# Two transformer blocks on one core: loads in order of use, squares spread out, a short norm, and the last updates shared with TensorE

## What is computed

```python
def rms_norm(x, g):                       # also rmsnorm
    y = xf * lax.rsqrt(jnp.mean(xf * xf, axis=-1, keepdims=True) + EPS)
    return y * g

h = x                                     # first block
hn = rms_norm(h, norm_g[0]); proj = hn @ w_in; ...
x = rms_norm(h, final_g)                  # end of the first block
xn = rmsnorm(x, norm_mix_pre)             # start of the second: two norms in a row
...
x = x + rmsnorm(mix_out, norm_mix_post)   # "the middle" below
hn = rmsnorm(x, norm_ffn_pre)
u = square(relu(hn @ w_up)); y = u @ w_down
x = x + rmsnorm(y, norm_ffn_post)         # the end
```

## Time and profile before

| what | value |
|---|---|
| median of 3 runs | 2653.14 us (2651.64 to 2653.33) |
| the profiled execution, its own time | 2653.11 us |
| its span | 2651.1 us |
| TensorE busy | 2606.0 us, 98% of the span |
| VectorE, ScalarE, GpSimd busy | 1609.6, 1217.0, 25.9 us |
| chain of work that ended last | TensorE 93%, VectorE 3%, ScalarE 1%, transfers 1% |

### The profile page before, as it was taken

How to read it: one execution, slowest core, us unless ns; L and a number is a source line. 1 busy time by engine, 2 the same in 40 slices (tenths; PEclk the granted TensorE clock), 3 DMA queues, 4 the chain that set the end, 5 groups by cost and what they waited for, 6 DMA issues and landing times.

```text
span 2651.1 us, 29862 instructions
## 1 busy us (share of the span) xinstructions
PE 2606.0 (98%) x11725; PEld 2160.2 (81%) x11725; DVE 1609.6 (61%) x1868; ACT 1217.0 (46%) x1471; POOL 25.9 (1%) x49
## 2 busy tenths in 40 slices
PE   7999999999999999999999999999999999999997
PEld 6888888888888888887888888888878888888886
DVE  4545665566657666766866666555576565565565
ACT  5554443444454444455444444444454344344443
POOL 1000000000000000000000000000000000000000
PEclk9999999999999999999999999999999999999999
DMA  6666766676765555677555666666657666676773
GB/s 216 206 193 194 212 197 198 193 212 195 220 201 174 170 166 166 191 227 210 160 181 176 182 183 183 200 198 207 216 161 220 196 203 215 188 218 206 200 221 121
DMA packets 437933, 515.39 MB, mean 194 GB/s; under 512 B 198416, under 2 KB 200576, under 8 KB 437792
## 3 DMA queue, kind: packets, MB, share of 16 engines
q1 hardware_dynamic: 434320, 504.45, 62.9%
q0 software_dynamic: 2384, 6.93, 1.0%
q10 hardware_dynamic: 1088, 2.10, 0.2%
HBM read 488.24 MB, written 2.10 MB: 185 GB/s over the span
## 4 chain that ended last, share of the span: by engine, by line
PE 93%; DVE 3%; ACT 1%; DMA 1%; issue 1%; SPq 1%; DVEq 0%; ACTq 0%
PE bank L33 92%; PE bank L36 1%; DMA t_stage<-in_a_w_in_dram 1%; DVE t_wl L51 1%; SPq L72 1%; DMA t_ytl<-t_pool 0%; ACT t_wh L42 0%; DVE t_pool L39 0%; ACT t_junk L42 0%; DVE t_pool L51 0%; DVE t_hres L54 0%; ACT t_pool L42 0%; DVE t_rq L51 0%; ACT t_yth L42 0%; DMA t_xtl<-t_pool 0%
## 5 line engine op out<-in xcount | busy, mean ns | idle before, releaser
L51 DVE TENSOR_TENSOR t_wl<-t_stage,t_wh 128x1024 fp32r<-128x1024 f32 x914 | 1102.6, 1220 | 694.7 <-ACT t_wh L42 693.1
L42 ACT ACTIVATE t_wh<-t_stage 128x1024 fp32r<-128x1024 f32 x914 | 953.6, 1056 | 839.7 <-PE bank L33 827.9
L33 PE MATMUL bank<-t_wl,t_xth 128*128 128x512 f32 x2496 | 989.1, 396 | 12.1 <-DVE t_xtl L54 6.3
L33 PE MATMUL bank<-t_wh,t_xtl 128*128 128x512 f32 x2496 | 975.8, 391 | 0.0
L33 PE MATMUL bank<-t_wh,t_xth 128*128 128x512 f32 x2496 | 975.0, 391 | 0.0
L33 PEld LDWEIGHTS bank<-t_wl,t_xth 128*128 128x128 f32 x2496 | 470.8, 189 | 108.6 <-DVE t_wl L51 7.0
L33 PEld LDWEIGHTS bank<-t_wh,t_xtl 128*128 128x128 f32 x2496 | 470.3, 188 | 99.6
L33 PEld LDWEIGHTS bank<-t_wh,t_xth 128*128 128x128 f32 x2496 | 471.0, 189 | 94.9 <-issue 0.2
L33 PE MATMUL bank<-t_wl,t_yth 128*128 128x512 f32 x1024 | 399.1, 390 | 0.0
L33 PE MATMUL bank<-t_wh,t_yth 128*128 128x512 f32 x1024 | 398.6, 389 | 0.0
L33 PE MATMUL bank<-t_wh,t_ytl 128*128 128x512 f32 x1024 | 398.5, 389 | 0.0
(11 more groups left out here) (185 smaller groups left out, 970.7 us busy)
## 6 DMA issues: line engine op xcount, KB each, us to landing
t_stage<-in_a_w_in_dram SPq DMA_DIRECT2D x192, 512.0 KB, 4.1
t_stage<-in_w_in_dram SPq DMA_DIRECT2D x178, 512.0 KB, 4.3
t_stage<-in_b_w_in_dram SPq DMA_DIRECT2D x128, 512.0 KB, 3.7
t_stage<-in_w_up_dram SPq DMA_DIRECT2D x128, 512.0 KB, 4.0
t_stage<-in_w_down_dram SPq DMA_DIRECT2D x128, 512.0 KB, 4.3
t_stage<-in_a_w_out_dram SPq DMA_DIRECT2D x64, 512.0 KB, 4.5
t_ytl<-t_pool SPq DMA_DIRECT2D x128, 128.0 KB, 3.2
t_stage<-in_b_w_out_dram SPq DMA_DIRECT2D x32, 512.0 KB, 5.3
```

What stands on the lines that cost most here:

```text
L33: return lambda e: e.matmul(*a, **k)
L42: return lambda e: e.activation(*a, **k)
L51: return lambda e: e.tensor_tensor(*a, **k)
```

## The change

It has four parts.

1. *Opening.* x is loaded by SyncE, its four pieces between the first five groups, each ahead of the groups that need it. TensorE gets four matmuls on a zeroed tile at the very start and three behind the first two turns (`busy_matmuls`); ScalarE gets one tiny copy at the start. Splits are issued one group ahead until group 5, then two, three, four (`ahead`). Group 0 begins with its four high x high matmuls, which need only the high part of the weights. The eight squares of x are four pieces; the first chunk's evacuation is a piece too. The 1 MB table is loaded behind the split of group 8.
2. *End of the first block.* Both norms come from one chain on four columns instead of two chains on two.
3. *Middle and end.* The last group of the last chunk does its six matmuls for i = 0 first, then those for i = 1 (`halves`), so that the half's square can start. Three chunks' sums are added up ahead (`partial_sum`); `short_norm` takes ScalarE's Sqrt, VectorE's reciprocal and one Newton step. Seven and five matmuls on constants follow the last real ones. In the middle, x is updated in pieces of 256 columns, and TensorE begins the next chunk when two pieces are turned instead of four.
4. *The last updates.* GpSimd has none. Three (i = 1 of columns 0, 1, 2) are made by TensorE: ahead of the last chunk it copies x into accumulators with three matmuls against the identity, and behind the norm it adds the sum times a diagonal matrix of the scale; ScalarE copies the results out. The other five stay on VectorE. The output goes in eight transfers of 256 KB, one of them from ScalarE's queue.

```diff
+    blank = pool4[:, 3, 0, 0:256]
+    c_blank = DV.do(lambda e: e.memset(blank, 0.0))
+    AC.do(lambda e: e.activation(junk[:, 0:64], blank[:, 0:64], ACT.Copy), c_blank)
+    def busy_matmuls(n):
+        for _ in range(n):
+            PE.run(lambda e: e.matmul(mbank[1][:, 0:256], blank[:, 0:128], blank, start=True, stop=True), c_blank)
...
-    for j in range(N_STAGE):
-        load_group(j)
+    load_group(0)
+    load_x(1)
+    load_group(1)
+    load_group(2)
+    load_x(2)
+    load_group(3)
+    load_group(4)
+    load_x(3)
+    def ahead(j):
+        return j + min(AHEAD, max(1, j - 4))
...
-            advance(j + AHEAD)
+            advance(ahead(j))
+            if j == 0:
+                need(lambda: 0 in ready and 1 in ready)
+                PE.wait(split_hi[0], *ready[0])
+                for kk in range(2):
+                    for i in range(2):
+                        PE.run(lambda e, o=acc[2 * pair + i], h=tokens(xh, kk, i), w=wh[:, 0, kk, :], f=kk == 0:
+                               e.matmul(o, h, w, start=f, stop=False))
+                PE.wait(split[0])
...
+            by_half = halves is not None and g == nk // 2 - 1
+            steps = [(kk, i) for i in range(2) for kk in range(2)] if by_half else \
+                [(kk, i) for kk in range(2) for i in range(2)]
...
+    def partial_sum(x, sums, n, width, marks):
+        m = DV.do(lambda e: e.tensor_reduce(x, sums[:, :, 0:n], AX, ALU.add), *marks)
+        return DV.do(lambda e: e.tensor_scalar(x, x, 1.0 / width, EPS, ALU.mult, ALU.add), m)
+    def short_norm(dst, x, part, last, width, marks):
+        a = rq[:, 0, 0:2]
+        m = DV.do(lambda e: e.scalar_tensor_tensor(out=x, in0=last, scalar=1.0 / width, in1=part,
+                                                   op0=ALU.mult, op1=ALU.add), *marks)
+        m = AC.do(lambda e: e.activation(a, x, ACT.Sqrt), m)
+        m = DV.do(lambda e: e.reciprocal(dst, a), m)
+        m = DV.do(lambda e: e.tensor_tensor(a, dst, x, ALU.mult), m)
+        m = DV.do(lambda e: e.scalar_tensor_tensor(out=a, in0=a, scalar=-0.5, in1=dst, op0=ALU.mult,
+                                                   op1=ALU.mult), m)
+        return DV.do(lambda e: e.scalar_tensor_tensor(out=dst, in0=a, scalar=1.5, in1=dst, op0=ALU.add,
+                                                      op1=ALU.mult), m)
...
-    pump()
-    pump()
+    turns[0]()
+    split_group(0)
+    load_group(5)
+    turns[1]()
+    busy_matmuls(2)
+    pool4_clear = PE.do(lambda e: e.matmul(mbank[1][:, 0:256], blank[:, 0:128], blank, start=True, stop=True))
+    temps.free[3] = (pool4_clear,)
+    later(*turns[2:])
...
-    later(x_norm)
+    later((x_square(0), 3), x_square(1), x_square(2), x_square(3), x_scale, first_evac)
...
-        m = norm_scale(s1, None, ssq, 4, D, (sq,))
-        m = DV.do(lambda e: e.tensor_tensor(s11, s1, s1, ALU.mult), m)
-        x2s = rq[:, 1, 2:4]
-        m = DV.do(lambda e: e.tensor_reduce(x2s, ssq2[:, :, 0:4], AX, ALU.add), m, sq2)
-        m = DV.do(lambda e: e.tensor_tensor(x2s, x2s, s11, ALU.mult), m)
-        m = DV.do(lambda e: e.tensor_scalar(x2s, x2s, 1.0 / D, EPS, ALU.mult, ALU.add), m)
-        m = rsqrt(s2, x2s, 2, (m,))
-        m = DV.do(lambda e: e.tensor_tensor(s12, s1, s2, ALU.mult), m)
+        m = DV.do(lambda e: e.tensor_reduce(v1, ssq[:, :, 0:4], AX, ALU.add), sq)
+        m = DV.do(lambda e: e.tensor_scalar(v1, v1, 1.0 / D, EPS, ALU.mult, ALU.add), m)
+        m = DV.do(lambda e: e.tensor_scalar(eps1, v1, EPS, None, ALU.mult), m)
+        m2 = DV.do(lambda e: e.tensor_reduce(v12, ssq2[:, :, 0:4], AX, ALU.add), sq2)
+        m = DV.do(lambda e: e.scalar_tensor_tensor(out=v12, in0=v12, scalar=1.0 / D, in1=eps1, op0=ALU.mult,
+                                                   op1=ALU.add), m, m2)
+        m = rsqrt(s12_1, both, 4, (m,))
...
+        if c == 3:
+            warm_n, warm, warm_free = misc.take()
+            for _ in range(7):
+                PE.run(lambda e: e.matmul(warm[:, 0:256], neg[:, 0:128], mask, start=True, stop=True), c_neg, c_mask,
+                       *warm_free)
...
+            if q == 3 and c == 2:
+                for n, (cc, i) in enumerate(by_pe):
+                    b = (tbank + mbank)[n]
+                    summed[cc, i] = b
+                    PE.run(lambda e, b=b, cc=cc, i=i: e.matmul(b, ident, hres[:, i, cols(cc)], start=True, stop=False),
+                           *trans.free[0], *trans.free[1], *misc.free[0], *misc.free[1], *sqf)
...
+    for _ in range(5):
+        PE.run(lambda e: e.matmul(acc[0][:, 0:256], neg[:, 0:128], mask, start=True, stop=True), *acc_free[0])
+    m_sD = short_norm(sD, xD, partD, ssq[:, :, 3], D, (sqd[-1], m_part))
...
+    for c, i in by_pe:
+        mm = PE.do(lambda e, c=c, i=i: e.matmul(summed[c, i], diag[:, i, :], drs[c][:, i, :], start=False, stop=True),
+                   m_diag[i], dr_marks[c, i])
+        d = dacc[:, i, cols(c)]
+        ready_out[c, i] = d, AC.do(lambda e, c=c, i=i, d=d: e.activation(d, summed[c, i], ACT.Copy), mm)
```

More of the change, by code:

```diff
@@ L336, in _program @@
                    s_g0, 16)
+    load_x(0)
     for i in range(2):
@@ L374, in slot @@
         return tile[:, n].rearrange("p a b -> p (a b)").rearrange("p (k n) -> p k n", n=width)
-    loaded, split, used = [], [], []
+    loaded, split, used, split_hi = [], [], [], []
     def load_group(j):
@@ L427, in proj @@
                 PE.wait(*ready[kt])
[L428 to L439, removed]
+                o = acc[2 * pair + i][:, 0:n]
+                h, l = tokens(xh, kt, i), tokens(xl, kt, i)
+                w_h, w_l = wh[:, j % N_SPLIT, kk, 0:n], wl[:, j % N_SPLIT, kk, 0:n]
+                first, last = k == 0, k == nk - 1
+                PE.run(lambda e, o=o, h=h, w=w_l, f=first: e.matmul(o, h, w, start=f, stop=False))
+                PE.run(lambda e, o=o, h=h, w=w_h: e.matmul(o, h, w, start=False, stop=False))
+                f = lambda e, o=o, l=l, w=w_h, t=last: e.matmul(o, l, w, start=False, stop=t)
+                if kk == 1 and (i == 1 or by_half):
+                    mark = PE.do(f)
+                    if by_half:
+                        halves.append(mark)
+                else:
+                    PE.run(f)
             used.append(mark)
@@ L495, in piece @@
                 ready[k] = ready[k + 1] = (v,)
-            later(piece)
+            steps.append(piece)
+        return steps
     turn_count = [0]
@@ L698, in _program @@
         sqv.append(last)
+    for c in range(8):
+        if c == 2:
+            need(lambda: (0, 1) in v_marks)
+        chunk = proj(xth, xtl, 0, x_ready)
+        if c == 0:
+            first_chunk += chunk
+        else:
+            v_evac(c, *chunk)
     m_sV = norm_scale(sV, None, ssq2, 8, GW, (sqv[-1],))
@@ L1562, in _program @@
                 rn, row, rmark = load_row(A["norm_ffn_post_2"][:, cols(c)])
-            pair, ps, m = proj(yth, ytl, 0, y_ready)
+            halves = [] if q == 3 and c == 3 else None
+            pair, ps, m = proj(yth, ytl, 0, y_ready, halves)
             if q == 3:
@@ new lines, in _program @@
+    for c, i in ((0, 0), (1, 0), (2, 0), (3, 0), (3, 1)):
+        h, d = hres[:, i, cols(c)], drs[c][:, i, :]
+        ready_out[c, i] = h, DV.do(lambda e, h=h, d=d, i=i: e.scalar_tensor_tensor(
+            out=h, in0=d, scalar=sD[:, i:i + 1], in1=h, op0=ALU.mult, op1=ALU.add), m_sD, dr_marks[c, i], sqf[-1])
+    order = ((0, 0), (1, 0), (0, 1), (2, 0), (1, 1), (3, 0), (2, 1), (3, 1))
+    for n, (c, i) in enumerate(order):
+        t, done = ready_out[c, i]
+        q = AC if (c, i) == by_pe[-1] else SP
+        end = q.dma(lambda e, c=c, i=i, t=t: e.dma_start(ov_[:, i, cols(c)], t), s_out, 16 * (n + 1), done)
```

169 lines of the change are left out of this document (101 added, 68 removed).

## The result

The changed kernel takes **2635.69 us** (median of 4 runs, 2632.58 to 2637.46) where the kernel before took 2652.68 us beside it (4 runs, 2651.64 to 2653.33): ratio 0.9935, 95% interval 0.9918 to 0.9952. That is 17.0 us faster; 23.4 were forecast, and 2635.69 lies in the range. The profiled execution took 2635.97 us, its span 2634.2, with TensorE busy for 2614.1 us of it.

What follows compares the result with a forecast made beforehand. The prediction took TensorE at 2.4 GHz as the bound, with gains only from waits, half-clock stretches and the tail. Terms 13.0 + 2.05 + 5.45 + 2.9 = 23.4 from 2653.11 gave 2629.7 us; range 2623 to 2638.

Steps and rivals of the forecast that it cites:

- Opening, 13.0 forecast: From the start to group 12: loads in order of use and splits one group ahead start group 12 13.0 us earlier.
- the one on the loads: In the opening: the second group's weights are there by 10 us, so group 1 starts at 12.5.
- the loads remain the bound: Rival for the opening: loads still limit it, gaining only 6 to 9 us, about 2635 us; chance 0.12.
- the band of the forecast itself: Whole kernel: the time lands in 2626 to 2632.5 us, with chance 0.50.
- Fill: Before group 0: matmuls on zeros raise the clock; the rival, chance 0.17, said they do not, giving 2633.6 us.
- Two norms from one chain, 2.05 forecast: Near 1238 us: 17 tiny operations instead of 30 end 2.05 us earlier, leaving a 1.4 us wait; no clock gain counted.
- Middle, 5.45 forecast: At the middle norm: first matmul 4.4 us earlier, full clock another 1.9, two later turns -0.9; 5.45 us.
- M: End of the last matmul ahead of the middle norm; the first matmul behind the norm was forecast 5.7 us later.
- a sign of error: After the middle: a wait in the groups behind the x squares would show the prediction wrong; no size given.
- End, 2.9 forecast: Behind the last matmul of the weights: 5.7 us less, minus 2.8 for three float32 matmuls ahead of the last chunk.
- E: End of the last matmul of the weights; the span was forecast to end 10.5 us later instead of 16.2.
- each of the eight output transfers pays its own start: Rival at the end: four more transfers cost 1.5 us each, giving 2635.7 us; chance 0.06.

Runs made afterwards that it cites:

- the base: The changed kernel with the small loads behind the split of group 2 and all eight last updates on VectorE; 2629.82 us, ratio 0.9911.

## Why the prediction was right and wrong

**Opening, 13.0 forecast, 6.3 measured: the step that failed.** It is the one on the loads, "even at the 259 GB/s of 8 to 12 us the 2.1 MB up to the second group's weights are there by 10". I took a rate measured with the small loads in it as a floor, and it fell to 170, so the weights came at 14.2 us. The rival that came true is "the loads remain the bound", priced at about 2635 us and given 0.12, with the very reason ("the small parameter loads still run"). The time lies in the stated range because the range covered this rival; the band of the forecast itself, 2626 to 2632.5, missed it. (The range's lower end was not reached by the bounds: all upper bounds together are 28.0 us, 2625.1.) The sign was in the trace: in the kernel before, 9 to 10 us showed

```profile
DMA packets 83, 0.12 MB, mean 124 GB/s; under 512 B 23, under 2 KB 23, under 8 KB 83
...
q0 software_dynamic: 23, 0.00, 42.3%
```

A share near 1 with a rate far under the 405 GB/s of the earlier trace rows meant here that the engines were busy with something small, and the next question is with what. Why the same small loads took 87% instead of 42% no run shows; in the kernel before, the large loads came in two queues. Most of the rest of the 6.7 us is the clock, which falls in the wait of 4.06 us and costs group 1 about 2.4. The other steps of the opening were right: with the small loads out of the way and the clock up (the run with a fill at 1470 us), groups 0, 2, 6 and 12 start at 8.39, 16.02, 29.20 and 45.67, forecast 8.6, 16.1, 28.8 and 45.2.

**Fill.** In the changed kernel it raised the clock before group 0, as forecast. It is not sure to: over eleven profiles with the same four matmuls, the first turns ran at the full pace in eight and at half in three.

**Two norms from one chain, 2.05 forecast, 2.0 measured**, and another 1.4 from the clock (the shift grows from 8.4 us at 1238.90 to 9.8 at 1242), which I left out because 1.4 us of waiting seemed nearer to the 1.95 us that dropped it than to the 0.71 that did not. Mis-sized, inside its bounds (3.5).

**Middle, 5.45 forecast, 4.5 measured.** The turns behind the first four groups come at 1948.86 before and 1932.91 after; less the shift at M and 0.9 us for two more turns, that is 5.6. Then TensorE waits at 1965 us, where it did not wait before:

```profile
1961.68 1.06 ACT L42 ACTIVATE t_yth<-t_ytl 128x1024 fp32r<-128x1024 f32 x1 [7.01 <-DMA t_ytl<-t_pool]
...
1965.18 0.50 PE L33 MATMUL bank<-t_wl,t_xth 128*128 128x512 f32 x1 [0.69 <-DVE t_wl L51]
```

The weights' low part stands on VectorE behind work on what ScalarE copies here, and this copy waits 7.01 us for a transfer of turned data (6.86 before). The squares of x, behind which the text lists a wait as a sign of error, end at 1947.9, well ahead of it. The wait takes back 1.1 us, a term that the sum did not have; all twelve kernels of the experiments wait here too, 0.5 to 0.9 us.

**End, 2.9 forecast**, measured 5.6 behind E less 2.6 to 2.7 ahead of it: 2.9 to 3.0. The size is right, the design was not questioned: I charged 2.8 us for the three sums and got E + 10.5 from the transfers alone (first ready at E + 3.45, 2.1 MB at 405 GB/s), so the sums did not stand in what set the end. By these very numbers the version without them ends 2.8 us earlier; the run showed 2.6. That each of the eight output transfers pays its own start did not show: the span ends at E + 10.6, and no run shows the 1.5 us that this rival charged.

**Small waits that moved**: near 1205 us TensorE waits 0.30 us where it did not, and near 1223 us 1.36 us for turned data where it waited 0.40. Together they cost some 1.8 us, while the wait at 1115 us no longer drops the clock, worth about 1.6. They cancel, as do the 1.4 us too little for the norms' clock and the 1.0 too much for the middle: that the sum misses by the opening alone is luck.

## What to carry to other kernels

Small loads can hold up large ones that come in another queue, so what is not needed at once belongs behind the first large loads: look for a stretch where the transfers' share is full and the rate is not, and for the packets that take the time. Before work is given to a second engine to shorten a tail, ask whether the tail is set by the transfers that follow it. A wait of 1 to 2.5 us is two costs, its length and perhaps the clock behind it. A few matmuls on constants in it can keep the clock; they won 1.9 us in the middle, and at 1470 us 1.2 to 1.6 against the base, in which the clock fell, at a price of 0.1 to 0.9 against runs in which it stayed. Whether they narrow the spread of the runs is not shown: the two versions with this fill spread over 0.9 and 2.1 us, the base over 2.6.

## What was not expected of the hardware

No single length of waiting decides whether the clock falls. At the place near 1470 us it stayed at 1.00 behind waits of 1.23 to 1.88 us (eight profiles, the kernel before among them) and fell behind 1.93, 2.05, 2.38 and 2.41 (0.83 to 0.86 over ten us); but at the place near 1110 us it fell behind 1.95 us in the kernel before (there at 1121) and behind 2.10 and 2.32 in two other profiles, and stayed behind 2.00 (twice), 2.23 and 2.34. What differs between them these runs don't show. Nor do they show why the same opening fill is early enough in one execution and not in the next. The wait at 1470 us itself varies because VectorE's work ahead of it comes behind a copy on ScalarE that waits for a transfer of turned data: 6.28 us in the changed kernel's profile, 6.67 in the base's and 7.13 in that of the run with the small loads late.
